# Leaving out the structural zeros in VectorE's products of triangular blocks

## The reference, cut to what matters

```
step(S): sa = S a_t;  S = S*w_t + sa b_t^T + v_t k_t^T;  y = S r_t      # 512 tokens, 2 directions, 8 heads of 64
```

## Time and profile before

| what | us |
|---|---|
| median of 3 runs | 1263.15 |
| the runs | 1263.0, 1263.15, 1283.46 |
| profiled execution, its own time | 1278.09 |
| its span | 1276.3 |
| TensorE busy (matmul) | 1191.9 |
| VectorE busy | 665.3 |
| ScalarE busy | 320.9 |
| GpSimd busy | 109.6 |

### The profile page before, as it was taken

One profiled execution on the slowest core, in us unless ns is written; L12 is line 12 of the kernel. 1 busy time (PEld: TensorE's weight loads), 2 busy tenths in 40 slices (PEclk: granted clock), 3 DMA queues, 4 the chain that ended last, 5 costly groups with the idle time before them and its releaser, 6 DMA issues.

```text
span 1276.3 us, 15428 instructions
## 1 busy us (share of the span) xinstructions
PE 1191.9 (93%) x6146; PEld 828.8 (65%) x6146; DVE 665.3 (52%) x1386; ACT 320.9 (25%) x714; POOL 109.6 (9%) x107
## 2 busy tenths in 40 slices
PE   4999999889688969899999999999999999999998
PEld 2545846676678669554647888844546568888643
DVE  2222105469966962769732656670397615656500
ACT  2212213665453240420311122110411321122100
POOL 0000100210101010125100000010054000000000
PEclk8899989989677976789999999999999999999999
DMA  9622312000001300163224745333522344553420
GB/s 358 229 91 96 132 67 70 1 1 1 3 1 67 109 19 34 51 247 130 67 66 134 237 137 188 137 135 111 198 84 74 124 132 132 161 169 132 152 79 33
DMA packets 96666, 140.06 MB, mean 110 GB/s; under 512 B 12207, under 2 KB 63058, under 8 KB 96466
## 3 DMA queue, kind: packets, MB, share of 16 engines
q1 hardware_dynamic: 95684, 136.84, 31.8%
q10 hardware_dynamic: 910, 2.22, 0.5%
HBM read 138.01 MB, written 1.05 MB: 109 GB/s over the span
## 4 chain that ended last, share of the span: by engine, by line
PE 78%; DVE 16%; ACT 2%; issue 2%; DMA 1%; POOL 0%; SPq 0%; DVEq 0%; ACTq 0%
PE bank L1209 24%; PE bank L1228 12%; PE bank L793 11%; PE bank L1048 4%; PE bank L1038 2%; PE bank L470 2%; PE bank L463 2%; DVE ring L1957 2%; DMA ring<-in_ada_w 1%; PE bank L982 1%; PE bank L625 1%; PE bank L1094 1%; PE bank L602 1%; PE bank L875 1%; DVE work L1959 1%
## 5 line engine op out<-in xcount | busy, mean ns | idle before, releaser
L1209 PE MATMUL bank<-work,ring 128*128 128x256 f32 x1024 | 222.7, 379 | 0.0
L1209 PEld LDWEIGHTS bank<-work,ring 128*128 128x128 f32 x1024 | 194.2, 190 | 26.2
L793 PE MATMUL bank<-work,ring 128*128 128x256 f32 (+2 forms) x448 | 147.0, 491 | 2.3 <-ACT work L1281 2.3
L793 PEld LDWEIGHTS bank<-work,ring 128*128 128x128 f32 (+1 forms) x448 | 85.9, 193 | 62.8 <-issue 55.7
L1228 PE MATMUL bank<-ring,work 128*128 128x512 f32 x288 | 124.3, 592 | 0.0
L1652 ACT ACTIVATE work<-work,prm 128x256 f32<-128x256 f32 x88 | 48.0, 592 | 250.5 <-DVE work L2501 224.0
L1228 PEld LDWEIGHTS bank<-ring,work 128*128 128x128 f32 x288 | 54.7, 190 | 68.0 <-issue 67.4
L2493 DVE TENSOR_TENSOR work<-bank,turned 128x512 f32<-128x512 f32 x44 | 30.4, 692 | 112.0 <-PE bank L1209 111.9
L1209 PE MATMUL bank<-work 128*128 128x256 f32 x384 | 83.9, 379 | 0.0
L1209 PEld LDWEIGHTS bank<-work 128*128 128x128 f32 x384 | 73.0, 190 | 9.9
L2511 DVE SCALAR_TENSOR_TENSOR work<-work,prm 128x256 f32<-128x256 f32 x176 | 77.1, 480 | 4.2 <-ACT work L1652 2.6
(11 more groups left out here) (430 smaller groups left out, 1781.8 us busy)
## 6 DMA issues: line engine op xcount, KB each, us to landing
ring<-in_w_up SPq DMA_DIRECT2D x32, 1024.0 KB, 7.8
ring<-in_w_in SPq DMA_DIRECT2D x24, 1024.0 KB, 7.5
ring<-in_w_down SPq DMA_DIRECT2D x16, 1024.0 KB, 6.3
ring<-in_ada_w SPq DMA_DIRECT2D x12, 1024.0 KB, 11.6
work<-in_w_up SPq DMA_DIRECT2D x12, 1024.0 KB, 7.7
ring<-in_w_out SPq DMA_DIRECT2D x10, 1024.0 KB, 6.1
work<-in_w_in SPq DMA_DIRECT2D x4, 1024.0 KB, 9.8
work<-in_w_down SPq DMA_DIRECT2D x4, 1024.0 KB, 6.0
```

Source lines behind the costliest of these rows:

```text
L793: ins = mm(b[0:rows, 0:toks], wt[:, k, off:off + rows], hT[:, k, 0:toks], start=(k == 0), stop=(k == KD - 1))
L1209: ins = mm(b[:, SEQ * half:SEQ * half + SEQ], wt[:, KD * half + k, P * j:P * j + P], xnT[:, k, :], start=(k == 0), stop=(k == KD - 1))
```

## The change

For b = 8 and b = 16 the products leave out terms that are zero by structure. In the first product, `upper`'s column c has entries in the rows from c on alone, so a pass takes four columns c to c+3, all b rows, and k from c to b-1. In the second, row i of `right` has entries up to column i alone, so a pass takes four rows and k from 0 to c+3. The passes thus sum over 16, 12, 8 and 4 values of k (b = 16) or 8 and 4 (b = 8) where each summed over all b. b = 8 goes in two passes where it went in one. For b = 4 the four TENSOR_TENSORs of a product are cut by pair of blocks and no longer by row, with as many elements. b = 2 is as it was. The steps of an inverse become four more (41 for group 0, 39 for group 1), and the numbers at which the asides stand are changed with them.

```diff
--- before.py
+++ after.py
@@ -1937,26 +1937,27 @@
                 step(V.transpose(sq_d, sq_c))
                 step(TC(block(t_inv, 32, 1), block(d_inv, 32, 1)))
                 for b in (2, 4, 8, 16):
-                    count = BLOCK // (2 * b)
+                    count, part = BLOCK // (2 * b), min(b, 4)
                     lower, upper, right = block(d_inv, 32 * b, b), block(t_inv, 0, b), block(t_inv, 33 * b, b)
-                    target = lower_t = block(t_inv, 32 * b, b)
-                    rows = b if b < 16 else 4
+                    target = block(t_inv, 32 * b, b)
                     inner_t, upper_t = (v[:, 0:count * b * b].rearrange("p (m j k) -> p m j k", m=count, j=b) for v in (xs_inv, turned))
                     step(TC(upper_t, upper.transpose([0, 1, 3, 2])))
-                    product = prod[:, 0:count * rows * b * b].rearrange("p (m i j k) -> p m i j k", m=count, i=rows, j=b)
-                    for left, other, dst in ((lower, upper_t, inner_t.transpose([0, 1, 3, 2])), (right, inner_t, target)):
-                        for r in range(0, b, rows):
-                            by_pair = count < b
-                            for q in range(count if by_pair else rows):
-                                if by_pair:
-                                    part, wide = product[:, q], [P, rows, b, b]
-                                    x, y = left[:, q, r:r + rows].unsqueeze(2), other[:, q].unsqueeze(1)
-                                else:
-                                    part, wide = product[:, :, q], [P, count, b, b]
-                                    x, y = left[:, :, q].unsqueeze(2), other
-                                ins = TT(part, x.to_broadcast(wide), y.to_broadcast(wide), MUL)
-                            step(ins)
-                            step(V.tensor_reduce(dst[:, :, r:r + rows], product, AX_X, ADD))
+
+                    def multiply(x, y, dst):
+                        i, j, k = x.shape[2], y.shape[2], x.shape[3]
+                        product = prod[:, 0:count * i * j * k].rearrange("p (m i j k) -> p m i j k", m=count, i=i, j=j)
+                        if count <= i:
+                            for q in range(count):
+                                ins = TT(product[:, q], x[:, q].unsqueeze(2).to_broadcast([P, i, j, k]), y[:, q].unsqueeze(1).to_broadcast([P, i, j, k]), MUL)
+                        else:
+                            for q in range(i):
+                                ins = TT(product[:, :, q], x[:, :, q].unsqueeze(2).to_broadcast([P, count, j, k]), y, MUL)
+                        step(ins)
+                        step(V.tensor_reduce(dst, product, AX_X, ADD))
+                    for c in range(0, b, part):
+                        multiply(lower[:, :, :, c:b], upper_t[:, :, c:c + part, c:b], inner_t.transpose([0, 1, 3, 2])[:, :, :, c:c + part])
+                    for c in range(0, b, part):
+                        multiply(right[:, :, c:c + part, 0:c + part], inner_t[:, :, :, 0:c + part], target[:, :, c:c + part])
                 t3 = t_inv[:, 0:1024].rearrange("p (x y) -> p x y", x=32)
                 step(V.transpose(sq_c.rearrange("p (n x) -> p x n", n=32), t3))
                 V.transpose(sq_d.rearrange("p (n y) -> p y n", n=32), t3.transpose([0, 2, 1])).then_inc(S["t_inv"], 1)
@@ -2028,7 +2029,7 @@
                     rates(n + 1)
 
             def maxima_between(step):
-                at = (3, 4, 8, 10, 12, 13, 14, 16, 18, 20, 22, 24, 26, 28, 30, 32)
+                at = (3, 4, 8, 10, 12, 14, 16, 18, 21, 23, 24, 26, 28, 30, 34, 37)
                 if step in at:
                     row_maximum(at.index(step))
             def state_steps(l):
@@ -2162,15 +2163,15 @@
                     scaled(n + 1)
 
             def states_between(step):
-                if step in (8, 10, 12, 13):
-                    q = (8, 10, 12, 13).index(step)
+                if step in (8, 10, 12, 14):
+                    q = (8, 10, 12, 14).index(step)
                     add_cross(q // 2, q % 2)
-                if step in (20, 22):
-                    take_state((step - 20) // 2)
-                if step in (24, 25):
-                    take_carry(step - 22)
-                if step in (28, 29):
-                    take_state(step - 26)
+                if step in (27, 29):
+                    take_state((step - 27) // 2)
+                if step in (31, 33):
+                    take_carry(2 + (step - 31) // 2)
+                if step in (37, 38):
+                    take_state(step - 35)
             invert(1, states_between)
             state_steps(0)
             join(1)
```

## The result

Twenty runs of the changed kernel have a median of 1260.07 us (1253.17 to 1268.03); twenty of the kernel before, 1273.17 us (1263.0 to 1283.46). The ratio is 0.991, 95% interval 0.9889 to 0.9932; it is taken without runs over 1.5% above the fastest of their kernel (four of the kernel before). Of 1273.17 us that is 11.5 us, with 8.7 to 14.1 as the interval: within the 2% that was called "no change", and clear of noise. The two medians themselves lie 13.1 us apart. The profiled execution took 1263.74 us with a span of 1261.9.

The account below looks back on a forecast made before the run. VectorE's inverse was taken to end last, with 3.6 and 7.0 us before TensorE would. Savings of 6.6 + 4.9 = 11.5 us from the median 1263.15 gave 1251.7 us; range 1243 to 1268, about 0.8.

Parts of the forecast that it names:

- no change: What a measurement cannot tell from an unchanged time: about 2%, 25 us; within it 0.93, faster 0.05, slower 0.02.
- The price of a pass: VectorE steps of the inverses: N elements cost 0.19 us plus 0.00104 us per element, products and reductions alike.
- rival 4: VectorE at half its rate in narrow slices, costing 6.4 us per inverse, as much as saved: 1263 us, chance 0.04.
- b = 16 and b = 8: VectorE's passes in each inverse: 6.38 us less for b = 16 and 0.16 us less for b = 8.
- First inverse: Inverse with the maxima: 6.6 us saved, all on the path, VectorE still last by 2.3 us.
- Second inverse: Slack of 7.0 us eaten, TensorE then ScalarE last, L1384 beginning at 448.6 instead of 453.50: 4.9 us saved.
- Rival 1: Second inverse's gain lost to a late `add_cross` or full bank holding `project_early`: 1256.6 us, chance 0.12.
- The clock: TensorE's granted clock behind the second inverse: effect taken as zero, bounds a 16 us gain and a 20 us loss.
- rival 2: TensorE keeps a higher clock once idleness before `join_quarters(1)` is gone: 1243.7 us with half, 1235.7 with all, chance 0.10.
- Rival 5: Whole kernel's runs come out at another level, near the profiled 1278.09: median 1266.6 to 1272 us, chance 0.17.

Follow-up runs that it names:

- e2: Changed kernel's steps, passes and asides, but each pass multiplies and sums all b terms, zeros too: median 1265.56 us, ratio 0.997 against the kernel before.
- e6: Changed kernel with zeros left out for b = 16 alone, b = 8 in one whole pass, asides at the old steps: 1255.61 us, ratio 0.9855 against before.
- e3: Zeros left out in the first inverse alone, the second with its asides as in the kernel before: median 1265.92 us, ratio 0.9941 against before.
- e4: Zeros left out in the second inverse alone, the first with its maxima as in the kernel before: median 1263.31 us, ratio 0.9952 against before.
- e7: Changed kernel with b = 16 in eight passes of two columns or rows instead of four passes: median 1264.24 us, ratio 0.9928 against before.
- e12: The kernel before, unchanged, run once more for its profile: one run of 1273.97 us.
- e5: Changed products, but asides at the step numbers of the kernel before: median 1259.25 us, ratio 0.9885 against before.
- e8: Changed kernel with take_state(0) and (1) earlier and the maxima from the eleventh on moved: 1254.15 us, ratio 0.9826 against before.
- e10: Changed kernel with the maxima and take_state(0), (1) moved, on the same chip as the changed kernel: 1254.22 us, ratio 0.9817 against before.
- e11: Changed kernel with the maxima and take_state(0), (1) moved, and the last add_cross one step earlier: 1253.31 us, ratio 0.9847 against before.

## Why the prediction was right, and where not

**The price of a pass** held to 8 ns for every size, narrow rows too: rival 4 is out.

**b = 16 and b = 8.** 6.38 + 0.16 us were forecast per inverse. VectorE's busy time in the first falls by 6.70 us (47.05 to 40.35), e2 and e6 divide it: b = 16 carries it, and b = 8 gives 0.25. The forecast's words for b = 8, four products and four reductions more, miscount: an inverse has four TENSOR_TENSORs and two reductions more (1386 VectorE instructions before, 1398 after, for two inverses). Its sum, 2.58 to 2.50 us, has the right ones.

**First inverse:** 6.6 forecast, 6.64 measured. It is VectorE's last transpose that ends last, with 2.08 us to TensorE (2.3 forecast).

**Second inverse:** 4.9 forecast, 4.77 measured, and the bound changed hands as forecast. Two parts on the way were off and cancelled. VectorE's end moved by 6.04 us and not 6.5, mostly since it waited 0.36 us longer for L703. Whether that is the change's is open: it waited 2.77 to 2.79 us in all profiles of the changed kernel and in e3, 2.42 in those of the kernel before and in e4, but 2.39 and 2.37 in e6 and e7. And TensorE was ready for L923 at 429.52, or 23.1 us behind the start, where 24.3 was worked out, because the last L705 took 1.09 us and not 1.84, and the matmuls behind it were faster too (granted clock 1.00 from 421 to 425 us, where the kernel before had 0.60 and 0.55); it then stood for `take_state(0)`, 1.88 us instead of 0.3. Rival 1 named that wait; it cost the end of the chain about as much as in the forecast.

**The clock** was taken as zero, and was not. First, a small part that belongs to the change: with no idleness in front of `join_quarters(1)`, the clock stays up for a while (0.88 in the 35 us from L1384, where it was 0.82; 0.90 in e4 and 0.83 in e3), and L661 takes 1.29 us. From L1384 to L982 it is 68.61 (e4) against 69.77 and 69.49, and 61.9 (changed) against 63.15 (e3): 0.9 to 1.3 us. That is rival 2 with its own mechanism, at a small part of its price. By the rule of the Trainium skill's page "TensorE: Matmul & The Clock Gate" (HAM oscillation) on idle gaps the trace agrees, to that extent. The mean of 0.70 over 69 us, on which the forecast rested rival 2, was no measure of the gap: most of the low clock in it is a stretch that begins 35 us later. That is the second part, and the larger. The same matmuls in the changed kernel and in e12:

```profile
484.65 2.88 PE L758 MATMUL bank<-work 128*64 128x128 f32 x16
487.46 2.18 PE L763 MATMUL bank<-work 128*128 128x64 f32 x16
489.57 1.58 PE L758 MATMUL bank<-work 128*64 128x128 f32 x16
```

```profile
487.46 2.88 PE L758 MATMUL bank<-work 128*64 128x128 f32 x16
490.27 3.68 PE L763 MATMUL bank<-work 128*128 128x64 f32 x16
493.88 2.88 PE L758 MATMUL bank<-work 128*64 128x128 f32 x16
```

The clock falls to 1.2 GHz in front of them in both, with no idleness of TensorE ahead of it (busy for 1.94 to 2.00 of every 2 us); in the changed kernel it is back soon after one L758, in e12 it is not when the second one ends. With the same second inverse, the stage is 6.3 to 6.8 us shorter where it comes back (e3 against the kernel before, the changed kernel against e4). It was short in nine profiles (changed three times, e3, e5, e6, e8, e10, e11) and long in five (before twice, e2, e4, e7). Every kernel with the wide first inverse had it long, nine of ten with a narrow one short; and e4, whose second inverse is the changed one, had it long, so the gap in front of `join_quarters(1)` is not its cause. That division points at the first inverse, but what would link it to a stretch 150 us later I can't say. If the long stretch always went with the kernel before, and the short one with the change, the times would have to fall by 11.4 + 1.2 + 6.5 = 19 us. By the ratios they fell by 11.5 (0.991), 11.8 (0.9907) and 20.3 us (0.9841) in three sets, by the medians by 13.1, 16.3 and 22.2; 19 is outside the first two intervals and inside the third.

The run times bound it. The shortest pieces of any profile with the long stretch (278.1 us to the first inverse, 240.6 for the stages less 1.6 between the inverses, 749.5 behind the first L982, and the 1.8 us by which a time exceeds its span) make 1268.4 us, an estimate. Of the kernel before, 4 of 20, 9 of 34 and 1 of 11 runs in the three sets are below that, so it can have the short stretch as well, unless another piece as large is in no profile. For the changed kernel the same sum with 6.5 us put in for the long stretch is 1255.9 us (no profile of it has one), and 4 of 20, 5 of 11 and 3 of 6 runs are below. **Open:** how often either kernel has the long stretch. So 11.4 us are shown, by the stages, to come from VectorE's shorter passes, and 0.9 to 1.3 from the clock behind the closed gap; up to 6.5 more, in some runs, is a stretch whose cause is not settled. Some 12.6 us lie inside the first two intervals, so the tenth in which 11.5 agrees was luck: the forecast left out the 1.2.

**The level.** Rival 5 (0.17) was the one to take seriously: 1263.15 was the median of three runs from a spread of 1262.5 to 1287, and the changed kernel's median came at 1260.07, between the forecast and that rival's 1266.6. The step that was off is the one that set the median of three runs as the base, 10.0 us below the median of twenty; the profiled execution (1278.09 - 11.5 = 1266.6) would have been 6.5 us off to the other side. The range held, since it reached there for this case.

## What to carry to other kernels

Where an engine's chain of vector instructions ends last, count elements and instructions separately: leaving out structural zeros pays as long as it saves more than the fixed cost of each step that it adds (here 0.19 us, or some 180 elements). b = 16 needed no step more, and b = 8 hardly earned its four. A gain is worth no more than the slack of the engine that comes next, so walk that one too: here 7 us of slack were just used up. And work placed between the steps of a chain has to be placed anew when the steps change in length: left at its old places it took back at least 3.4 of the 4.77 us of the second inverse (e5).

## What the runs showed of the hardware

The spread of a kernel's times, over 20 us, is made of pieces with levels of their own, and goes with TensorE's granted clock. In fourteen profiles the first inverse started between 278.1 and 288.0 us; the time between the inverses was 73.7 to 75.4; the stretch of 1.2 GHz above was worth 6.5; and from the first L982 to the end it took 749.5 to 749.9 or 752.7 to 753.1. Together that is 21 to 22 us, and the runs of the kernel before reach from 1262.53 to 1283.62 in the largest set. In that set the runs of 1262.5 to 1263.5 us have a mean granted clock of 0.953 or 0.954, those of 1283.2 to 1283.6 have 0.937 or 0.938. With such pieces a median of three runs is no base for a forecast of 1%; stages between fixed instructions, most of which repeat to 0.1 us, are.
